# A decoder layer on one core: the first x tile in two halves, squares shared anew between two engines, more ones products on TensorE

## The reference, cut to what matters

```
def rms_norm(x, w):
    xf = x.astype(jnp.float32)
    y = xf * lax.rsqrt(jnp.mean(xf * xf, axis=-1, keepdims=True) + EPS)
    return (y * w.astype(jnp.float32)).astype(x.dtype)

m, s_gla_new, s_hg_new = token_mix(rms_norm(x, norm_mix_pre[l]), w_in[l], ...)
h = x + rms_norm(m, norm_mix_post[l])
f = swiglu(rms_norm(h, norm_ffn_pre[l]), w_ffn_in[l], w_ffn_out[l])
return h + rms_norm(f, norm_ffn_post[l]), s_gla_new, s_hg_new
```

## Time and profile before

| | |
|---|---|
| median of 3 runs | 1041.59 us (1041.08 to 1041.91) |
| the profiled execution | 1041.37 us, of which 1039.6 us are the span of the trace |
| TensorE busy | 1028.8 us (99%) |
| VectorE busy | 688.2 us (66%) |
| ScalarE busy | 491.4 us (47%) |
| GpSimd busy | 64.8 us (6%) |
| granted TensorE clock | 1.00 in every slice |

### The profile page before, as it was taken

The page is one execution under the profiler, slowest core; times in us unless marked ns, Lnnn a source line. Parts: engine busy times, 40 slices in busy tenths (PEclk is TensorE's granted clock), DMA queues, the critical chain, the costliest instruction groups (busy, mean ns, idle before and its releaser), DMA issues.

```text
span 1039.6 us, 23593 instructions
## 1 busy us (share of the span) xinstructions
PE 1028.8 (99%) x10218; PEld 960.1 (92%) x10218; DVE 688.2 (66%) x1040; ACT 491.4 (47%) x775; POOL 64.8 (6%) x87
## 2 busy tenths in 40 slices
PE   7999999999999999999999999999999999999998
PEld 7989999989999899999899878999999999888886
DVE  6375745675726767357666578988888888744544
ACT  5533454632737335545327567644444444633532
POOL 6100003100013000031000000000000000000000
PEclk9999999999999999999999999999999999999999
DMA  7523224623227222345323281142432432422212
GB/s 200 176 69 83 62 74 121 184 62 83 73 62 223 82 64 62 93 126 160 83 62 93 87 294 36 51 113 81 117 87 82 112 92 62 143 84 86 86 50 91
DMA packets 130839, 105.28 MB, mean 101 GB/s; under 512 B 4304, under 2 KB 115920, under 8 KB 130736
## 3 DMA queue, kind: packets, MB, share of 16 engines
q1 hardware_dynamic: 125584, 85.68, 28.6%
q0 software_dynamic: 4864, 17.83, 5.6%
q10 hardware_dynamic: 288, 0.27, 0.1%
HBM read 91.96 MB, written 11.80 MB: 100 GB/s over the span
## 4 chain that ended last, share of the span: by engine, by line
PE 95%; DVE 2%; ACT 1%; DMA 0%; DVEq 0%; issue 0%; ACTq 0%; SPq 0%
PE ps L297 34%; PE ps L2086 23%; PE ps L2110 12%; PE ps L1303 10%; PE ps L417 3%; PE ps L1236 2%; PE ps L1211 1%; PE ps L1226 1%; PE ps L1238 1%; PE ps L1243 1%; PE ps L1275 1%; PE ps L1195 1%; PE ps L1157 1%; PE ps L1207 1%; PE ps L2121 1%; PE ps L2120 0%
## 5 line engine op out<-in xcount | busy, mean ns | idle before, releaser
L283 ACT ACTIVATE w_hi_t<-w_raw_t 128x1024 fp32r<-128x1024 f32 x73 | 77.1, 1057 | 253.3 <-PE ps L297 171.1
L297 PE MATMUL ps<-x_hi,w_lo_t 128*128 128x288 f32 x880 | 192.0, 300 | 0.0
L297 PE MATMUL ps<-x_hi,w_hi_t 128*128 128x288 f32 x880 | 188.3, 296 | 0.0
L297 PE MATMUL ps<-x_lo,w_hi_t 128*128 128x288 f32 x880 | 188.1, 295 | 0.0
L287 DVE TENSOR_TENSOR w_lo_t<-w_raw_t,w_hi_t 128x1024 fp32r<-128x1024 f32 x73 | 89.0, 1220 | 127.1 <-ACT w_hi_t L283 125.9
L297 PEld LDWEIGHTS ps<-x_hi,w_lo_t 128*128 128x128 f32 x880 | 140.8, 189 | 2.9 <-issue 1.0
L297 PEld LDWEIGHTS ps<-x_lo,w_hi_t 128*128 128x128 f32 x880 | 141.6, 189 | 0.0
L297 PEld LDWEIGHTS ps<-x_hi,w_hi_t 128*128 128x128 f32 x880 | 141.6, 188 | 0.0
L2086 PE MATMUL ps<-x_hi,w_lo_t 128*128 128x288 f32 x276 | 81.5, 295 | 0.0
L2086 PE MATMUL ps<-x_lo,w_hi_t 128*128 128x288 f32 x276 | 81.4, 295 | 0.0
L2086 PE MATMUL ps<-x_hi,w_hi_t 128*128 128x288 f32 x276 | 81.3, 295 | 0.0
(11 more groups left out here) (386 smaller groups left out, 2336.2 us busy)
## 6 DMA issues: line engine op xcount, KB each, us to landing
w_raw_t<-in_w_in_dram SPq DMA_DIRECT2D x57, 512.0 KB, 3.8
merged<-in_w_ffn_in_dram SPq DMA_DIRECT2D x22, 512.0 KB, 5.1
w_raw_t<-in_w_ffn_in_dram SPq DMA_DIRECT2D x22, 512.0 KB, 4.4
w_raw_t<-in_w_ffn_out_dram SPq DMA_DIRECT2D x22, 512.0 KB, 3.6
w_raw_t<-in_w_in_dram SPq DMA_DIRECT2D x32, 256.0 KB, 3.9
h_t<-in_x_prompt_dram SPq DMA_DIRECT2D x8, 512.0 KB, 5.5
h_t<-in_state_gla_dram POOLq DMA_DIRECT2D x4, 1024.0 KB, 6.1
h_t<-in_state_hgrn_dram POOLq DMA_DIRECT2D x8, 512.0 KB, 8.2
```

Source lines behind the costliest of these rows:

```text
L283: nc.scalar.activation(w_hi_t[:, u % NSPL, 0:nk, :], w_raw_t[:, u % NRAW, 0:nk, :], ACT.Copy).then_inc(w_hi, 1)
L297: m = nc.tensor.matmul(out[:, q, :], w[:, u % NSPL, k, :], x(k, q), start=first and i == 0, stop=last and i == len(todo) - 1)
```

## The change

Four things are changed, all in the opening.

1. SP loads x tile 0 as two transfers of 512 columns each, with a semaphore of its own for the second (`x_back_in`).
2. ACT sums the squares of tile 0 in two halves. The first half's sum is brought into the form sum/1024 + eps by a small instruction, and enters the logarithm of the second as its bias. ACT also sums all of tile 1, which DVE did before, and the first 704 columns of tile 2.
3. DVE no longer starts with the squares of tile 1. It scales tile 0 first, then sums the last 320 columns of tile 2 and brings them into the form sum/1024 + eps (one small `tensor_scalar`), and then scales tiles 1 and 2.
4. TensorE runs eight ones products as its first work (they wait only for the tile of ones), then the gain transposes, then eight ones products where four stood. The four behind the turned tiles stay.

```diff
+X_BACK = D - 320
@@ SP
+            if c == 0:
+                sp.dma_start(xt[c][:, 0:HALF], xp_v[c][:, 0:HALF]).then_inc(x_in[c], 16)
+                sp.dma_start(xt[c][:, HALF:D], xp_v[c][:, HALF:D]).then_inc(x_back_in, 16)
+                continue
             sp.dma_start(xt[c][0:tok(c), :], xp_v[c] if c < NC else xs_v).then_inc(x_in[c], 16)
@@ ACT
-        def square_sum(c):
+        def square_sum(c, cols=slice(0, D), out=None):
             n = tok(c)
-            act.wait_ge(x_in[c], 16)
-            act.activation(square[0:n, :], xt[c][0:n, :], ACT.Square, accum_out=stat[0:n, 0, c:c + 1])
+            act.activation(square[0:n, cols], xt[c][0:n, cols], ACT.Square, accum_out=stat[0:n, 0, c:c + 1] if out is None else out)
 
-        def inverse_root(c0, c1):
-            n = tok(c0)
+        def inverse_root(c, sum_of, base):
+            n = tok(c)
             act.drain()
-            act.activation(stat[0:n, 1, c0:c1], stat[0:n, 0, c0:c1], ACT.Ln, scale=1.0 / D, bias=eps_c[0:n, :])
+            act.activation(stat[0:n, 1, c:c + 1], sum_of, ACT.Ln, scale=1.0 / D, bias=base)
             act.drain()
-            act.activation(stat[0:n, 1, c0:c1], stat[0:n, 1, c0:c1], ACT.Exp, scale=-0.5).then_inc(squared, c1 - c0)
+            act.activation(stat[0:n, 1, c:c + 1], stat[0:n, 1, c:c + 1], ACT.Exp, scale=-0.5).then_inc(squared, 1)
+
+        def whole_root(c):
+            act.wait_ge(x_in[c], 16)
+            square_sum(c)
+            inverse_root(c, stat[0:tok(c), 0, c:c + 1], eps_c[0:tok(c), :])
...
-        square_sum(0)
-        inverse_root(0, 1)
-        act.wait_ge(sum_1, 1)
-        inverse_root(1, 2)
-        square_sum(2)
-        inverse_root(2, 3)
+        act.wait_ge(x_in[0], 16)
+        square_sum(0, slice(0, HALF))
+        act.drain()
+        act.activation(lb[:, 0, 0:1], stat[:, 0, 0:1], ACT.Identity, scale=1.0 / D, bias=eps_c[:, :])
+        act.wait_ge(x_back_in, 16)
+        square_sum(0, slice(HALF, D), lb[:, 4, 0:1])
+        inverse_root(0, lb[:, 4, 0:1], lb[:, 0, 0:1])
+        whole_root(1)
+        act.wait_ge(x_in[2], 16)
+        square_sum(2, slice(0, X_BACK))
+        act.wait_ge(back_sum, 1)
+        inverse_root(2, stat[:, 0, 2:3], lb[:, 0, 1:2])
@@ DVE
-        dve.wait_ge(x_in[1], 16)
-        dve.drain()
-        dve.scalar_tensor_tensor(square_1, xt[1], 1.0, xt[1], ALU.mult, ALU.mult, accum_out=stat[:, 0, 1:2]).then_inc(sum_1, 1)
         dve.wait_ge(gain_row, 1)
+        dve.wait_ge(x_back_in, 16)
         scale_x(0)
+        dve.wait_ge(x_in[2], 16)
+        dve.scalar_tensor_tensor(square_back[:, X_BACK:D], xt[2][:, X_BACK:D], 1.0, xt[2][:, X_BACK:D], ALU.mult, ALU.mult, accum_out=lb[:, 4, 1:2])
+        dve.drain()
+        dve.tensor_scalar(lb[:, 0, 1:2], lb[:, 4, 1:2], 1.0 / D, EPS, ALU.mult, ALU.add).then_inc(back_sum, 1)
         scale_x(1)
         scale_x(2)
@@ TensorE
+        def ones_products(n):
+            for _ in range(n):
+                nc.tensor.matmul(ps[:, 0, 0:P], ones[:, :], ones[:, :], start=True, stop=True)
+
+        pe.wait_ge(consts, 2)
+        ones_products(8)
         pe.wait_ge(gain_in, 16)
         pe.wait_ge(consts, 5)
...
-        for _ in range(4):
-            nc.tensor.matmul(ps[:, 0, 0:P], ones[:, :], ones[:, :], start=True, stop=True)
+        ones_products(8)
         turn_x(0)
         turn_x(1)
         turn_x(2)
         pe.wait_ge(x_lo_s, 1)
-        for _ in range(4):
-            nc.tensor.matmul(ps[:, 0, 0:P], ones[:, :], ones[:, :], start=True, stop=True)
+        ones_products(4)
```

19 lines of the change are left out of this document (9 added, 10 removed).

## The result

The changed kernel takes 1043.86 us (median of 13 runs, 1042.45 to 1045.14), where the kernel before takes 1041.59 on the same chip (13 runs, 1041.08 to 1042.07). The ratio is 1.0021, with an interval of 1.0014 to 1.0028: a loss of 2.3 us. The prediction was 1041.5 us, with a range of 1040.8 to 1042.2, and it gave slower a chance of 0.03. It was wrong.

What follows compares the result with a forecast made beforehand. VectorE's work in the opening was taken to set the first product on x at 13.59. Starting rest parts 0.10 us sooner gave 1041.37 - 0.1 = 1041.3, and 1041.5 us with the median 0.2 above the profiled run; range 1040.8 to 1042.2.

Steps and rivals of the forecast that it cites:

- later issues are hidden behind transfers: Opening loads on SP: one more load takes 0.4 us to issue, hidden behind data of 1.3 us per tile.
- cut off: Rival at the first unit: a larger gain, but unit 1's weight lands late and nothing is left, 1041.6 us; chance 0.08.
- the second half only after the first: Rival on tile 0's load: second half lands at 7.1, 2.15 us lost, 1043.7 us; chance 0.02.
- The rule that spoke against the change: Skill's DMA rule for loads: at least 1 MiB each, coalesce small ones; its 2.0 us fixed cost would give 1043.2.
- TensorE falls back to the slow pace: Rival on the first products on x: 3.6 us of them at half pace, 1.8 us lost, 1043.4 us; chance 0.02.
- The reading of the clock: TensorE in the opening: granted clock reads full, 2.4 GHz, while early rows stand 0.22 to 0.23 us apart.
- lower bound 3.9: Earliest start for ScalarE's first square, if first bytes come sooner than the mean rate says; gain then 0.25 us.
- the root: ScalarE's result for tile 0, needed by its scaling: ready 2.25 us after the first square starts, at 6.30.
- the gain row: Rival on TensorE's gain transposes: slow pace delays the first scaling to 6.88, 0.44 us lost, 1042.0 us; chance 0.22.
- conflict with GpSimd: Rival on VectorE's small instruction: it meets GpSimd's first cast on the shared port, 1.0 us lost, 1042.6 us; chance 0.01.
- s + 4.33: VectorE's first rest part, 4.33 us after the first scaling starts (s, 6.34): 10.67, where it was 10.77.
- The slack at the first unit: GpSimd's split of unit 1 ends at 16.07, TensorE needs it at 16.56: allows a gain up to 0.45 us.

Runs made afterwards that it cites:

- experiment 1: The kernel before with only x tile 0 loaded in two halves, both waited for by every user: 1044.48 us, ratio 1.0022.
- experiment 4: The changed kernel run again without edits, for a second profile: 1044.38 us, ratio 1.0024.
- experiment 5: The changed kernel with tile 0 cut by tokens into two loads of 64 whole rows, both waited for: 1043.82 us, ratio 1.0022.
- experiment 13: The kernel before with tile 0 loaded in two halves and the gains' load moved to SP's queue behind them: 1044.15 us, ratio 1.0025.
- experiment 14: The kernel before with tile 0 loaded in four loads of 256 columns: 1044.77 us, ratio 1.0028.
- experiment 7: The kernel before with tile 1, not tile 0, loaded in two halves, both waited for: 1042.59 us, ratio 1.0007.
- experiment 10: The kernel before with a 4 KB load put ahead of tile 0 on SP's queue: 1043.28 us, ratio 1.0013.
- experiment 12: The kernel before with SP issuing tile 1 only once tile 0 has landed: 1045.21 us, ratio 1.0032.
- experiment 6: The changed kernel with the second half of tile 0 issued from ScalarE's queue, behind the gains' load: 1042.75 us, ratio 1.0009.
- experiment 3: The kernel before with only the new ones products, eight first and eight where four stood: 1041.78 us, ratio 0.9998.
- experiment 9: The changed kernel with 14 more ones products between the turning of tiles 0 and 1: 1044.13 us, ratio 1.0022.
- experiment 15: The changed kernel with eight more ones products between the turning of tiles 0 and 1: 1043.79 us, ratio 1.0021.
- experiment 2: The changed kernel with tile 0 loaded whole again: 1042.61 us, ratio 1.0008.
- experiment 16: The changed kernel with the whole load of tile 1 issued by ScalarE, behind the gains: 1042.70 us, ratio 1.0009.
- experiment 8: The changed kernel with tiles 1 to 3 loaded in halves too: 1043.60 us, ratio 1.0017.

## Why the prediction was wrong

**The step that failed** is in the part on the load: SP issues one more load, and "later issues are hidden behind transfers". From it came tile 1 at 5.87, tile 2 at 7.2 and the weight of unit 1 where it was. The reasoning was about the time at which SP issues, and there it held: tile 1 is issued at 1.71 and its bytes have their turn from 4.4 on. What it left out is that a load is there only with the last of its 16 signals. With short loads ahead on the same queue, the last one or two signals come about 2 us late (after, and experiments 1, 4, 5, 13 and, more spread, 14), and so they do in every load that follows. Splitting tile 1, a 4 KB load ahead, a forced pause, or a half on another queue don't do it in the executions profiled (experiments 7, 10, 12, 6). No rival of the prediction had this: "cut off" had the weight of unit 1 late, but no tile. The nearest, the second half only after the first, priced the right kind of loss at 2.15 us with the wrong load late: the second half lands at 4.4, and the tile behind it is the late one.

**The rule that spoke against the change** was quoted and set aside for a reason that held but wasn't enough. The Trainium skill, DMA: Bandwidth & Descriptors, Rules for kernel authors, asks for loads of 1 MiB and more. The prediction argued that a fixed cost would be overlapped, and it is: the halves land 0.7 us apart. The measured loss of experiment 1 is in accord with the advice, but it isn't a fixed cost added to each load.

**A second cost that was held to be nearly impossible** follows from the first. "TensorE falls back to the slow pace" had a chance of 0.02, because the waits would be short. With a wait of 2.87 us it happened, in the granted clock itself: 0.50 from about 12.0 to 15.4. It fell on the turnings and not on the products, and so it cost less than the 1.8 us of that rival: of the 2.40 us it is about 0.5, by which the three rest parts take longer. Experiment 13 shows the difference, with tile 1 as late, the clock at 1.00 and the rest parts at their old 2.68. In experiment 12, 0.8 us stand behind the landing.

**The reading of the clock.** The prediction says that the granted clock reads full ahead of 8.46 while the pace is slow. The view prints 1.00 also where the trace has no record of the clock, and its first record, at full clock, is at 8.56 in the kernel before, where the pace rises. It is at 5.17 after, at 4.39 in experiment 3, at 10.03 in experiment 7 and at 14.44 in experiment 10, each time about where the fast rows begin. Ahead of it the 1.00 is no reading. The pace there, 0.22 to 0.24 us a row, is near that of the stretch at 0.50 after (3.32 / 16 = 0.21). Nothing in the forecast hung on this.

**Points that held.** The first square of 512 columns at 3.80 (4.05 predicted, lower bound 3.9); from it to the root 2.33 us (2.25); the first scaling at 6.28 (6.34); the gain transposes ended at 6.0 (6.0 to 6.3), so the gain row wasn't late; the squares of 320 columns with the small instruction took 0.65 (0.67), with the latter at 0.15 and no conflict with GpSimd. From a first scaling at 6.28, s + 4.33 gives a rest part at 10.61, where before it was 10.77: with the tiles on time, that would have been a gain of 0.16 us. No run shows it, because none had both the first half at 3.8 and tiles 1 and 2 on time; the nearest, experiment 9, has tile 2 at 8.05 and a filler in the way.

**The slack at the first unit** was named: GpSimd's split "takes it all if that weight lands over 0.4 us later". That weight landed at 15.5, 3.0 us later than before (12.5), and the split, by GpSimd's timeline, ended just ahead of TensorE's 19.23:

```profile
15.56 1.04 POOL L510 CAST w_hi_t<-w_raw_t 128x1024 fp32r<-128x1024 f32 x1 [1.79 <-DMA w_raw_t<-in_w_in_dram]
16.68 2.39 POOL L512 TENSOR_TENSOR w_lo_t<-w_raw_t,w_hi_t 128x1024 fp32r<-128x1024 f32 x1
```

So even with tiles 1 and 2 on time, this late weight alone would have held the first unit until 19.1, some 2.5 us behind before. Experiment 15 shows the same from the other side: its first product is 1.6 us sooner than after, and half of that is lost again in the wait for this weight.

**The three parts of the change, by their price.** The split alone costs 1.0022 (experiment 1); the new order of squares with a whole load 1.0008, with an interval that just takes in no change (experiment 2); the ones products nothing (experiment 3). The first two don't add up to the whole, 1.0021 to 1.0024; that both wait for the same late tiles would explain it, but no run tests it.

**What stays open.** What is shown is that splitting the first load brings the late tile (experiment 1), and that whole loads on the same queue don't (experiments 2 and 3). Why one or two engines fall behind, and which ones, isn't shown: the trace has the signals and some long packets, not a cause. Half rows and the gains' load on the other queue are ruled out, since the lag is there without them (experiments 5 and 13). The number of loads, a short load at the head, and a dry queue are made unlikely by experiments 7, 10 and 12, each with one profiled execution. Experiment 9 has tile 1 on time with the changed kernel's own loads, so an execution without the lag proves little. For experiments 7 and 10 the profiled execution lies within 0.15 us of the median, and other rows account for most of its loss; in experiments 12 and 16 it is the fastest of its runs, and there it could be luck. Why experiment 8, with all loads short, has the lag milder isn't explained.

## What to carry to other kernels

Splitting the first of several queued loads moves the loads behind it too; ask of each of them what it costs if it lands 2 us later, before counting the 0.7 us that the split brings. A landing is the last of 16 signals, so read the last two of a load, and not only its rate. Where such a delay leaves TensorE idle for some us, as here, count the clock that it may lose behind it, and then look at the next load in the queue, which is late too. And look where the profiled execution lies among its runs before concluding from what it doesn't show.
